# Expert weights in a mixture-of-experts stage: whole matrices of 16 KB per partition instead of 8 KB halves

## What is computed

```python
# t: 256 rows of 1024; 32 experts, top 2 of them per token; w_gate, w_up: 1024 x 512; w_down: 512 x 1024
for e in range(N_EXPERTS):
    hid = jax.nn.silu(t @ w_gate[e]) * (t @ w_up[e])
    out = out + combine[:, e:e + 1] * (hid @ w_down[e]).astype(F32)
```

## Time and profile before

| what | value |
|---|---|
| time, median of 3 runs | 2008.85 us (2008.83 to 2010.33) |
| the profiled execution, from its first to its last instruction | 2004.9 us |
| TensorE busy / VectorE / ScalarE | 1875.0 us (94%) / 1163.1 us (58%) / 817.7 us (41%) |
| expert products (lines 1507 and 1525) busy | 193.7 us and 102.7 us |
| TensorE idle ahead of them for DMA | 53.5 us and 29.9 us |
| moved by DMA | 453.4 MB |

### The profile page before, as it was taken

The page is one execution under the profiler, slowest core; times in us unless marked ns, Lnnn a source line. Parts: engine busy times, 40 slices in busy tenths (PEclk is TensorE's granted clock), DMA queues, the critical chain, the costliest instruction groups (busy, mean ns, idle before and its releaser), DMA issues.

```text
span 2004.9 us, 29967 instructions
## 1 busy us (share of the span) xinstructions
PE 1875.0 (94%) x12368; PEld 1413.5 (71%) x12368; DVE 1163.1 (58%) x1492; ACT 817.7 (41%) x1015; POOL 57.9 (3%) x47
## 2 busy tenths in 40 slices
PE   7999999977777778999999999999999999999998
PEld 5445757544444444788898888888888888788887
DVE  6988656533333334555678385556655678385554
ACT  4234532222222222534368465333534467555331
POOL 2430000000000000000000000000000000000000
PEclk9999999989999988999999999999999999999999
DMA  6334438999999999555454355644655454364652
GB/s 245 105 105 129 165 137 359 382 421 420 420 420 420 420 420 370 198 186 189 148 185 152 128 186 171 211 164 165 217 168 200 151 177 151 122 209 150 209 168 105
DMA packets 160441, 453.40 MB, mean 226 GB/s; under 512 B 9601, under 2 KB 21121, under 8 KB 135729
## 3 DMA queue, kind: packets, MB, share of 16 engines
q1 hardware_dynamic: 158480, 447.65, 60.6%
q10 hardware_dynamic: 1616, 3.24, 0.5%
q0 software_dynamic: 208, 0.59, 0.1%
HBM read 544.78 MB, written 1.05 MB: 272 GB/s over the span
## 4 chain that ended last, share of the span: by engine, by line
PE 73%; DMA 16%; DVE 6%; ACT 2%; issue 1%; POOL 0%; SPq 0%; ACTq 0%; DVEq 0%; POOLq 0%
PE ps L1016 23%; PE ps L1026 17%; PE ps L1025 17%; DMA ring<-in_w_down 13%; DMA ring<-in_w_up 3%; PE ps L1184 3%; PE ps L1507 2%; PE ps L1525 2%; PE ps L1486 1%; DVE xn L2546 1%; PE ps L1152 1%; PE ps L1153 1%; DVE W L2551 1%; DVE xn L2540 1%; DVE W L2553 1%
## 5 line engine op out<-in xcount | busy, mean ns | idle before, releaser
L2345 DVE TENSOR_TENSOR w_lo<-raw,w_hi 128x2048 fp32r<-128x2048 f32 x152 | 333.8, 2208 | 125.6 <-ACT w_hi L1830 118.3
L1830 ACT ACTIVATE w_hi<-raw 128x2048 fp32r<-128x2048 f32 x152 | 279.8, 1850 | 227.0 <-PE ps L1016 197.0
L1026 PE MATMUL ps<-w_hi,a_lo 128*128 128x512 f32 (+1 forms) x976 | 368.4, 378 | 0.0
L1016 PE MATMUL ps<-w_hi,a_hi 128*128 128x512 f32 (+1 forms) x928 | 353.9, 381 | 0.2 <-DVEq L2385 0.2
L1025 PE MATMUL ps<-w_lo,a_hi 128*128 128x512 f32 (+1 forms) x912 | 343.3, 376 | 0.0
L1507 PE MATMUL ps<-ring,W 128*32 128x256 f32 x3008 | 193.7, 407 | 56.4 <-DMA ring<-in_w_up 53.5
L1026 PEld LDWEIGHTS ps<-w_hi,a_lo 128*128 128x128 f32 x976 | 183.6, 188 | 34.2
L1016 PEld LDWEIGHTS ps<-w_hi,a_hi 128*128 128x128 f32 x928 | 174.7, 188 | 33.3 <-issue 2.4
L1507 PEld LDWEIGHTS ps<-ring,W 128*32 128x32 f32 x3008 | 96.1, 115 | 140.0 <-DMA ring<-in_w_up 64.4
L1025 PEld LDWEIGHTS ps<-w_lo,a_hi 128*128 128x128 f32 x912 | 171.8, 188 | 30.1
L2345 DVE TENSOR_TENSOR y_lo<-raw,y_hi 128x2048 fp32r<-128x2048 f32 x50 | 114.6, 2291 | 48.5 <-ACT y_hi L1830 45.9
(11 more groups left out here) (450 smaller groups left out, 2817.8 us busy)
## 6 DMA issues: line engine op xcount, KB each, us to landing
ring<-in_w_gate SPq DMA_DIRECT2D x94, 1024.0 KB, 23.0
ring<-in_w_up SPq DMA_DIRECT2D x94, 1024.0 KB, 26.7
ring<-in_w_down SPq DMA_DIRECT2D x94, 1024.0 KB, 22.1
raw<-in_w_in SPq DMA_DIRECT2D x57, 1024.0 KB, 5.1
raw<-in_ffn_w_up SPq DMA_DIRECT2D x44, 1024.0 KB, 5.2
raw<-in_ffn_w_gate SPq DMA_DIRECT2D x42, 1024.0 KB, 5.1
raw<-in_ffn_w_down SPq DMA_DIRECT2D x40, 1024.0 KB, 6.1
raw<-in_w_out SPq DMA_DIRECT2D x10, 1024.0 KB, 5.0
```

Of the source, the lines that this page charges most:

```text
L1016: return released(pe.matmul(dst, a, b, skip_group_check=True, **kw))
L1026: return pe.matmul(dst, a_l, b_h, start=False, stop=final, skip_group_check=True)
L1830: act.activation(E.hi_view(name, ahead), E.raw_view(name, ahead), ACT.Copy).then_inc(hi_split, 1)
L2345: tt(E.lo_view(name, ahead), E.raw_view(name, ahead), E.hi_view(name, ahead).bitcast(F32), ALU.subtract)\
```

## The change

The ring of nine becomes three gate-and-up slots of 32 KB per partition and three down slots of 16 KB, the same 18.9 MB. Tile q uses number q mod 3 of each. Gate and up are loaded as whole matrices, one DMA of 2 MB with 128 rows of 16 KB each; partition p then holds rows 8p to 8p+7. Down is one such DMA in slots 0 and 1 and two DMAs of 8 KB rows in slot 2, whose two pieces of memory do not touch. TensorE waits once for both matrices of a gate-and-up. The signal at the end of a first half is gone, and a load of gate-and-up waits for all of the gate-and-up three tiles back. The order of the loads is gate, up, down of the same tile, and a late tile's waits stand in it as before. The early load of the first pair is gone. `xn` gets its columns as 128 k + s from 8 s + k over the full 1024, and three of the buffers that hold `wo` weights change places.

```diff
+HI_SLOT = [0, 1, 2, 0, 1, 2, 1, 0, 2, 1]
...
+        for i, (gate_at, up_at) in enumerate((("y", "X0"), ("raw0", "raw2"), ("hi1", "lo0"))):
...
+        for i, (first_at, second_at) in enumerate((("W1", "W2"), ("lo2", "a_hi"), ("a_lo", "W0"))):
...
-            def load_pair(n, halves, cond=None):
-
-                if n < RING:
-                    sp.wait_ge(unit_used, ring_freed_by[n])
-                    if n == 2:
-                        sp.wait_ge(done["rows"], marks["rows"].number(("m", 1, 1), {}) + 1)
+            def load_gate(q, e, cond=None):
+
+                if q >= STAGES:
+                    sp.wait_ge(expert_used, E.pair_number(("gu", q - STAGES)) + 1)
+                sp.dma_start(gu_ring[q % STAGES][:, 0:2 * UNIT], load_expert("w_gate", e, KB), cond=cond)\
+                    .then_inc(gate_up_loaded[q % STAGES], 16)
...
+            def load_down(q, e, cond=None):
+
+                if q >= STAGES:
+                    sp.wait_ge(expert_used, E.pair_number(("d", q - STAGES)) + 1)
+                dst, src, at = down_ring[q % STAGES], load_expert("w_down", e, SIDES), down_gap[q % STAGES]
+                if at == UNIT:
+                    sp.dma_start(dst[:, 0:2 * UNIT], src, cond=cond).then_inc(down_loaded[q % STAGES], 16)
                 else:
-                    sp.wait_ge(expert_used, n + 1 - RING)
-                for at, src in zip(ring_at[n % RING], halves):
-                    sp.dma_start(ring[n % RING][:, at:at + UNIT], src, cond=cond).then_inc(expert_loaded[n % RING], 16)
...
-                if units.at[name][0] + 1 == gates_used + PRE_RAW:
-                    load_gate_up(0, 0, halves=(0,))
...
-            load_gate_up(0, 0, halves=(1,))
-            load_gate_up(1, 1)
-            load_down(0, 0)
-            load_gate_up(2, FIXED_AT.index(2))
+            sp.wait_ge(unit_used, PRE_UNITS - 4)
+            load_gate(0, 0)
+            sp.wait_ge(done["rows"], marks["rows"].number(("m", 1, 1), {}) + 1)
+            load_up(0, 0)
+            load_down(0, 0)
+            sp.wait_ge(unit_used, PRE_UNITS - 3)
+            load_gate(1, 1)
+            sp.wait_ge(unit_used, PRE_UNITS - 2)
+            load_up(1, 1)
+            sp.wait_ge(unit_used, PRE_UNITS)
+            load_gate(2, 2)
+            load_up(2, 2)
+            load_down(1, 1)
+            load_down(2, 2)
...
-            for q in range(1, TILES):
+            for q in range(STAGES, TILES):
+                if q in LATE_AT:
+                    late_known(LATE_AT.index(q))
+                load_gate(q, expert_of(q), used_of(q))
+                load_up(q, expert_of(q), used_of(q))
                 load_down(q, expert_of(q), used_of(q))
-                if q + 2 in LATE_AT:
-                    late_known(LATE_AT.index(q + 2))
-                if q + 2 < TILES:
-                    load_gate_up(q + 2, expert_of(q + 2), used_of(q + 2))
-            sp.wait_ge(expert_used, E.pair_number(("gu", LAST, 1)) + 1)
+            sp.wait_ge(expert_used, E.pair_number(("gu", LAST - 1)) + 1)
...
-                    slot = landed(E.pair_number(("gu", q, half)))
-                    row = ring_gap[slot] + UNIT
+                    if half == 0:
+                        pe.wait_ge(gate_up_loaded[stage], q // STAGES * 32 + 32)
...
-                    if half == 0:
-                        m.then_inc(expert_used, 1)
...
-                ins = tt(xn[:, t, part].rearrange("p (k s) -> p k s", k=4), by_part(x_sb[:, t, part]),
-                         gain_row[:, part].rearrange("p (k s) -> p k s", k=4), ALU.mult)
+                ins = tt(part_of(xn[:, t, :], c), by_part(x_sb[:, t, part]), part_of(gain_row, c), ALU.mult)
```

More of the change, by code:

```diff
@@ L42 @@
 PAIRS = -(-TILES // 2)
-RING = 9
+STAGES = 3
 LAYERS = 2
@@ L357, in tile_period @@
         if q + 1 < TILES:
-            for half in range(2):
-                tiles.event(("gu", q + 1, half))
+            tiles.event(("gu", q + 1))
             fill(("gu", q + 1), 0)
@@ L376, in plan @@
         mark("gathered", (0, i))
-    for half in range(2):
-        tiles.event(("gu", 0, half))
+    tiles.event(("gu", 0))
     fill(("gu", 0), 1)
@@ L471, in plan @@
     assert RAW == 3 and all(n % RAW == 0 for n in units.per.values()), units.per
-    assert tiles.n == 3 * TILES
+    assert tiles.n == 2 * TILES
     return units, shape, banks, bank_of, marks, tiles
@@ L732, in bass_hybrid_moe_then_swa_gla @@
         pre_loaded = [semaphore(f"pre_loaded{i}") for i in range(PRE_RAW)]
-        expert_loaded = [semaphore(f"expert_loaded{i}") for i in range(RING)]
+        gate_up_loaded = [semaphore(f"gate_up_loaded{i}") for i in range(STAGES)]
+        down_loaded = [semaphore(f"down_loaded{i}") for i in range(STAGES)]
         expert_used = semaphore("expert_used")
@@ L922, in load_gate_up, with load_expert @@
[L922 to L933, removed]
+            def load_expert(m, e, k):
+                return A[m][0][e, :, :].rearrange("(p k) n -> p (k n)", k=k)
@@ L1488, in gather @@
                 fill(m, ("G", g, i))
-            def landed(n):
-                pe.wait_ge(expert_loaded[n % RING], n // RING * 32 + 32)
-                return n % RING
             def expert_gate_up(q):
-                dst = bank(("gu", q))
+                dst, stage = bank(("gu", q)), q % STAGES
+                row = gu_gap[stage] + 2 * UNIT
                 for half in range(2):
@@ L1500, in expert_gate_up @@
                         pe.wait_ge(done["gathered"], nth("gathered", (0, half)))
-                    slot = landed(E.pair_number(("gu", q, half)))
-                    row = ring_gap[slot] + UNIT
+                    if half == 0:
+                        pe.wait_ge(gate_up_loaded[stage], q // STAGES * 32 + 32)
                     for j in range(4):
-                        a = packed_rows[q // GROUP_TILES % 2][:, 4 * half + j, SLOTS_OF[q] % GROUP_TILES, :]
+                        kb = 4 * half + j
+                        a = packed_rows[q // GROUP_TILES % 2][:, kb, SLOTS_OF[q] % GROUP_TILES, :]
                         for c in range(SIDES):
-                            w = bass.AP(ring[slot][:, 0:1].tensor, 512 * j + P * c, [[row, P], [ring_gap[slot], 2], [1, P]])
+                            w = bass.AP(gu_ring[stage][:, 0:1].tensor, 512 * kb + P * c, [[row, P], [gu_gap[stage], 2], [1, P]])
                             m = pe.matmul(dst[SLOTS * c:SLOTS * c + SLOTS, 0:SEQ].rearrange("p (a n) -> p a n", n=P), a, w,
@@ L1511, in expert_gate_up @@
                                 m.then_inc(expert_used, 1)
-                    if half == 0:
-                        m.then_inc(expert_used, 1)
                 fill(m, ("gu", q))
             def expert_down(q):
-                dst = bank(("ey", q))
-                slot = landed(E.pair_number(("d", q)))
+                dst, stage = bank(("ey", q)), q % STAGES
+                pe.wait_ge(down_loaded[stage], (q // STAGES + 1) * (16 if down_gap[stage] == UNIT else 32))
                 for f in range(SIDES):
@@ L1523, in expert_down @@
                         rows = quad_rows(r, h, q)[0]
-                        at = ring_at[slot][f // 2] + f % 2 * D + 512 * r + SEQ * h
-                        m = pe.matmul(dst[rows, 0:SEQ], hidT[q % 2][:, f, :], ring[slot][:, at:at + SEQ], start=f == 0, stop=f == SIDES - 1,
-                                      skip_group_check=True, tile_position=(0, rows.start))
+                        at = f // 2 * down_gap[stage] + f % 2 * D + 512 * r + SEQ * h
+                        m = pe.matmul(dst[rows, 0:SEQ], hidT[q % 2][:, f, :], down_ring[stage][:, at:at + SEQ],
+                                      start=f == 0, stop=f == SIDES - 1, skip_group_check=True, tile_position=(0, rows.start))
                         if f == c == 0:
@@ L1834, in hi1 @@
                 n0 = PRE_SPLIT.index(name)
-                if n0 >= RAW:
-                    act.wait_ge(unit_used, E.unit_value(PRE_SPLIT[n0 - RAW]) + 1)
+                earlier = [i for i in range(n0) if HI_SLOT[i] == HI_SLOT[n0]]
+                if earlier:
+                    act.wait_ge(unit_used, E.unit_value(PRE_SPLIT[earlier[-1]]) + 1)
                 act.wait_ge(pre_loaded[E.pre_slot(name)], units.at[name][0] // PRE_RAW * 16 + 16)
```

44 lines of the change are left out of this document (27 added, 17 removed).

## The result

The kernel after takes 2020.14 us (median of 4 runs, 2017.43 to 2021.19) against 2008.86 before: a ratio of 1.0056 with a 95% interval of 1.0045 to 1.0068, so it is slower by 11.3 us. The forecast was 2006.9 with a range up to 2016. The profiled execution of after has a span of 2019.3 us, 14.4 more than the one of before.

What follows compares the result with a forecast made beforehand. The expert stage was taken as bound by bytes, the dense layers by TensorE. Larger rows -4.9, start +2.8, tail +0.1, steady run and `xn` nothing, sum to -2.0 us: 2006.9 us, range 2000 to 2016.

Steps and rivals of the forecast that it cites:

- Part 3: Steady run of the expert stage: costs nothing, as the queue never runs dry, with a margin of about 2.5 us.
- rival A: Late tile's wait in the steady run: the queue runs dry in every round, slower, 2021 us; chance 0.18.
- part 2: Start of the expert loads: tile 5 goes out late into an empty queue, +2.8 us.
- rival D: Expert loads: each load has a price of its own, so fewer loads are much faster, 1841 us; chance 0.02.
- Part 1: Expert weight loads: larger rows of 16 KB raise the rate to 426 GB/s, -4.9 us.
- Part 4: Tail, last gate-and-up (tile 46): TensorE waits for the whole matrix, not the second half, +0.1 us; other end +1.8.
- Rival C: Expert weight loads: engines cut 16 KB rows into what they had, so larger rows gain zero, 2011.8 us; chance 0.10.
- rival B: Expert weight loads: a 16 KB row is worth more, 12.0 us, so 1999.8 us; chance 0.14.
- Part 5: Rows of `xn`: reads 8 elements apart cost nothing more; 0.5 us if cost grew with distance.

Runs made afterwards that it cites:

- e12: The changed kernel with the signal of a used down put half of a gate-and-up's products later; 2056.67 us, ratio to before 1.0241.
- e11: The changed kernel with the signal of a used down put a quarter of a gate-and-up's products later; 2037.30 us, ratio to before 1.0141.
- e4: The changed kernel with loads in the order of use, gate-and-up of q, then down of q-1; 2008.28 us, ratio to before 0.9993.
- e5: The changed kernel with the signal of a used down moved earlier, to the first gather or scatter product behind it; 2008.09 us, ratio to before 0.9997.
- e8: The kernel of e4 with each load of 16 KB rows made as two of 8 KB rows; 2010.23 us, ratio to before 1.0011.
- e2: The changed kernel with every load of 16 KB rows made as two of 8 KB rows; 2021.79 us, ratio to before 1.0061.
- e3: The kernel before with only the new load order, gate-and-up of q, then down of q, waits unchanged; 2012.00 us, ratio to before 1.0018.
- e7: The kernel before with TensorE waiting for both halves of a gate-and-up, load order as before; 2010.46 us, ratio to before 1.0008.

## Why the prediction was wrong

**Part 3 failed: "The margin is about 2.5 us"**, and with it the sentence of rival A that engines ahead of the slowest may run dry for nothing. The place and the wait were right; both sides of the margin were off, the larger by far "In the queue is then one down, 2 MB, 5.0 us". By the order of the program it is. In e12, where the queue runs dry before new bytes come, one can read what is left of the down when tile 6 has landed, at 399.92, until the gate goes out at 404.67:

```profile
GB/s 414 276 552 414 552 414 276 276 552 690 276 414 276 552 276 552 414 276 276 0 276 138 138 138 138 0 0 138 0 138 0 0 138 0 0 0 0 0 0 0
DMA packets 81, 1.07 MB, mean 224 GB/s; under 512 B 16, under 2 KB 16, under 8 KB 16
```

Only 1.07 of 2.10 MB starts behind the landing, and over 22 rounds of e11 and e12 it is 0.9 to 1.3 MB, 1.1 on the average: 2.6 us at 425 GB/s in place of 5.0, and some 2.9 with the rows under way at the landing (an estimate: half a row of 16 KB on each of 16 engines). The rate falls off some 2.3 us behind the landing, when the first engines are through, and the last bytes start 3.9 us behind it. The way against it was 1.9 us and what the signal of landing takes; in the traces it is 0.14 (landing to first product, from the chain below) + 1.19 (to the gate's issue, for which I had 0.98) + 0.96 (to the first byte: e12's gate, issued at 404.67, for which I had 0.9) = 2.3 us. So some 0.3 to 0.6 us are left and not 2.5, and none for the engines that are through first.

The first byte is not the end of it either. A load of 2 MB landed 7.8 us after its issue in e12, 2.9 over its bytes at 425 GB/s, where my own part 2 had 7.4 - 5.0 = 2.4 for 8 KB rows; 0.96 of it goes by before the first byte, and part 3 counted that alone. The rest, I take it, is a slow start and the wait for the slowest engine; no run separates them.

```profile
437.81 20.38 DMA gu_ring<-in_w_up
458.19 0.14 issue
458.32 5.22 PE ps L1518 x64
```

By the Trainium skill (DMA: Bandwidth & Descriptors, Anatomy of one DMA) a transfer that GpSimd issues costs 2.0 us beside its bytes (the prediction did not say that the figure is for GpSimd's path); for these loads of SyncE the runs show 2.4 and 2.9 when nothing lies ahead, and nothing visible when the queue is full, as the prediction said of rival D.

**Rival A was the case**, at 2021 us for its "some 1 us goes 14 times"; the time is 2020.1. It had 0.18. But its condition, a way of over 5 us, was not met: the way was 2.3 us, and what it ran against was half of what rival A, too, took to be queued. That its sum lands so near is in part luck: the 14 rounds make up some 11 us of it, and parts 1, 2 and 4 missed in both directions.

**Part 1 (-4.9)** stands in its rate, forecast 426, measured 425 (e4) and 424 (e5) against 420 (e8). In time it is worth 2.0 us between the medians of e4 and e8, 2.7 by the landing of tile 46, and 1.65 in the dry queue (e2). The term was over-sized, and in after it hid part of the loss. Rival C (420 GB/s) and rival B (over 430) are out by the same rates.

**Part 2 (+2.8)** had the issue right: 366.5 forecast and 368.23 measured, of which 1.7 is the late start. But the up of tile 5 landed 14.2 us after the gate's issue (TensorE starts on it at 382.52), not 12.4: this gate took 9.2 us to land, with nothing ahead of it, where I had 7.4. The length of the rows is not why: in e2, with 8 KB rows, the same tile landed 13.9 us after the gate's issue. By the traces the part is 382.4 - 376.15 - 1.7 = +4.6. e3, which has this order and 8 KB rows, is 2.8 us above before.

**Part 4 (+0.1)** came out at its other end, +1.8, and one cost was missing: the last down at the lower clock, +1.5. I had taken 12 us of work between the landings of tiles 44 and 46 as reason enough for the higher level. In after TensorE stood idle 3.92 us ahead of tile 46, and its 64 products took 5.35; in e4, e5 and e8, behind an idle 1.5 to 1.9, they took 3.66. e7 puts the whole wait alone at 1.3 us.

**Part 5 (nothing)** held. The writes of `xn` in after:

```profile
L2849 DVE TENSOR_TENSOR xn<-x_sb,W x4: 1082/1134/1154, 314.2 to 332.8; 128x512 f32<-128x512 f32 x4
```

1.13 us against 1.07, 0.06 of the 0.5 that a cost growing with the distance would have been.

**Still open** is how the 0.8 us of a round divides between engines that stand still and rows that start slowly: the views give the 16 engines together. Open too is how much of the down's missing half moves because most engines are ahead of the slowest, and how much while the signal of landing is on its way.

## What to carry to other kernels

When one queue serves loads in program order, ask for each wait in it how many bytes still have to move when it ends. Read that from a trace: here it was half of what the program's order says, since the rest had moved before TensorE could act on the landing. Compare it with the way from that landing to the new load's full rate, not to its first byte. A coarser wait on the consumer and a later wait in the queue can each be nearly free and cost 11 us together, so they are to be costed together. Put the signal that frees a buffer on the first instruction behind its last use that itself waits for nothing that the same queue brings.

## What was not expected of the hardware

A load of 2 MB took 7.8 us from issue to landing (the median of e12; 9.2 in the round of tile 4 in after) with little or nothing ahead of it, 2.9 us over its bytes at 425 GB/s, while a full queue hides all of it. The DMA share hardly shows such gaps: after still reads 0.99 and e2 1.00; the GB/s column does, 412 against 424. From 398 to 402 us the engines of after count as 91.5% busy while they move 336 of 425 GB/s, 79%: the rows there take longer. And doubling the row from 8 to 16 KB still brought 1.2% of rate at 420 GB/s, though in time only about half of what that rate is worth, 2.0 to 2.7 us of 4.9.
